# Experts in five teams of 128 token slots, with 4 KB and 8 KB weight runs

## The reference

```python
logits = xf @ router_w + router_b            # 256 tokens, 8 experts
top_logit, top_e = lax.top_k(logits, 2)
top_w = softmax(top_logit)
def expert_block(args):                      # D 1024, D_FF_EXPERT 3584
    tok_b, e = args
    xb = xf[tok_b]
    return (silu(xb @ wg[e]) * (xb @ wu[e])) @ wd[e]
out = zeros((T, D)).at[row_tok].add(y * row_w[:, None])
```

## Time and profile before

| | us |
|---|---|
| median of 3 runs (lowest, highest) | 1687.45 (1686.11, 1691.96) |
| the profiled execution, its own time | 1692.91 |
| its span, first to last instruction | 1691.1 |
| expert part: first weight load issued | 722.2 |
| first expert product | 732.7 |
| last down product's records end | 1676.0 |
| last addition into x ends | 1684.8 |

### The profile page before, as it was taken

How to read it: one execution, slowest core, us unless ns; L and a number is a source line. 1 busy time by engine, 2 the same in 40 slices (tenths; PEclk the granted TensorE clock), 3 DMA queues, 4 the chain that set the end, 5 groups by cost and what they waited for, 6 DMA issues and landing times.

```text
span 1691.1 us, 16145 instructions
## 1 busy us (share of the span) xinstructions
PE 1611.1 (95%) x6482; PEld 868.2 (51%) x6482; DVE 480.8 (28%) x953; ACT 199.0 (12%) x439; POOL 0.9 (0%) x7
## 2 busy tenths in 40 slices
PE   3999989999989999789999999999999999999997
PEld 2566755555546667554454444454444444444443
DVE  6577733434343644330110011100111000111002
ACT  1123230000011233200010000000000000000000
POOL 0000000000000000000000000000000000000000
PEclk9999899999999999789999999999999999999999
DMA  9935625888762100099999998999999989999993
GB/s 347 327 109 199 236 87 174 277 294 290 286 233 96 58 1 1 1 345 395 392 368 391 392 392 332 387 341 389 388 359 370 386 337 389 392 359 361 392 392 125
DMA packets 222010, 481.53 MB, mean 285 GB/s; under 512 B 15816, under 2 KB 33608, under 8 KB 221936
## 3 DMA queue, kind: packets, MB, share of 16 engines
q1 hardware_dynamic: 220488, 478.64, 76.8%
q10 hardware_dynamic: 1448, 1.84, 0.5%
HBM read 479.41 MB, written 1.06 MB: 284 GB/s over the span
## 4 chain that ended last, share of the span: by engine, by line
PE 91%; DMA 3%; DVE 2%; SPq 2%; ACT 1%; issue 1%; DVEq 0%; ACTq 0%
PE bank L1209 31%; PE bank L1238 16%; PE bank L1204 11%; PE bank L971 7%; PE bank L1230 6%; PE bank L962 4%; PE bank L1178 3%; PE bank L1216 2%; DMA ring<-in_ada_w 1%; DMA ring<-in_moe_wg 1%; PE bank L1284 1%; PE bank L1300 1%; PE bank L1098 1%; DVE ada_acc L1412 1%; PE bank L952 1%; SPq L607 1%
## 5 line engine op out<-in xcount | busy, mean ns | idle before, releaser
L1209 PE MATMUL bank<-ring,h_T 128*128 128x512 f32 (+1 forms) x896 | 355.3, 550 | 3.8 <-ACT h_T L727 1.3
L1238 PE MATMUL bank<-ring,m_qk_T 128*128 128x512 f32 x624 | 277.7, 597 | 0.7 <-ACT m_qk_T L843 0.7
L1209 PEld LDWEIGHTS bank<-ring,h_T 128*128 128x128 f32 x896 | 167.8, 191 | 165.2 <-issue 114.7
L1209 PE MATMUL bank<-ring,cmp_region 128*128 128x512 f32 x448 | 197.1, 593 | 0.0
L1238 PEld LDWEIGHTS bank<-ring,m_qk_T 128*128 128x128 f32 x624 | 116.2, 190 | 144.8 <-issue 140.9
L1763 DVE SCALAR_TENSOR_TENSOR m_s_region<-s_v,bank 128x512 f32<-128x512 f32 (+1 forms) x70 | 39.1, 558 | 489.8 <-ACT s_v L836 353.2
L836 ACT ACTIVATE s_v<-bank 128x512 f32<-128x512 f32 (+1 forms) x70 | 34.5, 493 | 997.5 <-PE bank L1209 654.1
L1209 PEld LDWEIGHTS bank<-ring,cmp_region 128*128 128x128 f32 x448 | 83.7, 190 | 99.6 <-issue 99.6
L1767 DVE SCALAR_TENSOR_TENSOR m_s_region<-m_s_region,bank 128x512 f32<-128x512 f32 (+1 forms) x70 | 39.1, 558 | 317.6 <-PE bank L1209 224.3
L971 PE MATMUL bank<-ring,h_T 128*128 128x512 f32 (+1 forms) x320 | 117.6, 517 | 0.0
L1204 PE MATMUL bank<-ring,h_T 128*64 128x256 f32 x896 | 102.4, 381 | 1.0 <-DVE m_s_region L1767 1.0
(11 more groups left out here) (314 smaller groups left out, 1022.0 us busy)
## 6 DMA issues: line engine op xcount, KB each, us to landing
ring<-in_moe_wg SPq DMA_DIRECT2D x56, 2048.0 KB, 9.7
ring<-in_moe_wu SPq DMA_DIRECT2D x56, 2048.0 KB, 15.5
ring<-in_moe_wd SPq DMA_DIRECT2D x56, 2048.0 KB, 19.1
ring<-in_ada_w SPq DMA_DIRECT2D x28, 1024.0 KB, 8.9
ring<-in_ada_w SPq DMA_DIRECT2D x10, 2048.0 KB, 14.4
ring<-in_w_in SPq DMA_DIRECT2D x10, 2048.0 KB, 12.1
ring<-in_ffn_wg SPq DMA_DIRECT2D x6, 1536.0 KB, 10.4
ring<-in_ffn_wu SPq DMA_DIRECT2D x6, 1536.0 KB, 9.4
```

What stands on the lines that cost most here:

```text
L1209: last = mm(ps[4 + part][:, 0:w], xT[st.into][:, k, 128 * st.tile:128 * st.tile + 128], view_at(slot, w)[:, k, :], start=k == 0, stop=k == ...
L1238: last = mm(ps[st.y + half][:, :], hbT[:, j % 2, 128 * q:128 * q + 128], down_at(st.slots[2], st.w)[:, q, 512 * half:512 * half + 512], st ...
```

## The change

1. Experts go in five **teams** that fill 128 slots: one expert (128), two (96 + 32), one (128), two (96 + 32), two (64 + 64), by rank of count (0), (2, 7), (1), (3, 6), (4, 5). Instead of two steps a unit, PE computes one team at a time; each product of a k-step is issued once for each lane of array columns: one lane of 128, or lanes of at most 64 (0 to 64, 64 to 96, 96 to 128 in the 96 + 32 teams; 0 to 64, 64 to 128 in the last).
2. Work goes in **stages** of two units (the last of one). Gate and up loads take 512 rows by 1024 columns (4 KB runs), down loads two neighbouring rows per partition (8 KB runs); the hidden columns are transposed with a stride of 2 to match. The number and size of loads stay: 168 of 2 MB.
3. The scatter weights tokens in the picks themselves (`onehot_weighted`), one bank at a time, four products a team; the gather is 128 columns wide; releases move into the products and the ACT and DVE steps; the pair loop on SP is unrolled. `OVER` is 4; slot ranks and capacities are set by POOL.
4. The first four modulation chunks are summed half on DVE (four slices), half on PE (four products of 512 columns against `cond` spread over 128 columns), with one product that adds DVE's half; DVE takes the diagonal of the result.

```diff
-OVER = 3
+OVER = 4
+TEAMS = (((0, 0, 128),), ((1, 0, 96), (2, 96, 128)), ((3, 0, 128),), ((4, 0, 96), (5, 96, 128)), ((6, 0, 64), (7, 64, 128)))
+SLOT_RANK, SLOT_CAP = (0, 2, 7, 1, 3, 6, 4, 5), (128, 96, 32, 128, 96, 32, 64, 64)
+SPANS = ((0, 2), (1024, 2), (2048, 2), (3072, 1))
...
+        self.lanes = [(m, a, min(a + (128 if c1 - c0 == 128 else 64), c1)) for m, (_, c0, c1) in enumerate(TEAMS[team])
+                      for a in range(c0, c1, 128 if c1 - c0 == 128 else 64)]
...
+    for j in range(len(STAGES) + 1):
+        if j < len(STAGES):
+            for part in range(2):
+                for piece in range(STAGES[j].units):
+                    add(STAGES[j], part, piece)
+        if j:
+            for unit in range(STAGES[j - 1].units):
+                add(STAGES[j - 1], 2, unit)
...
+            for n, (st, part, piece, m) in enumerate(MOE_LOADS):
+                e, slot = expert_id(st.team, m), n % RING
...
+                sp.wait_ge(ring_free[slot], FREED[slot] + n // RING)
+                if part == 2:
+                    f0 = st.f0 + 512 * piece
+                    sp.dma_start(ring[:, slot, :].rearrange("p (g n) -> p g n", g=2),
+                                 w[f0:f0 + 512, :].rearrange("(g p f) n -> p g (f n)", p=128, f=2)).then_inc(ring_full[slot], 16)
+                elif st.units == 2:
+                    sp.dma_start(wide_at(slot), w[512 * piece:512 * piece + 512, st.f0:st.f0 + 1024].rearrange("(k p) n -> p k n", p=128)).then_inc(ring_full[slot], 16)
...
+            for e in range(N_EXP):
+                do(nc.gpsimd.memset(slot_rank[:, e:e + 1], float(SLOT_RANK[e])))
+                do(nc.gpsimd.memset(slot_cap[:, e:e + 1], float(SLOT_CAP[e])))
...
+            def ada_half_product(c):
...
+                w = slot_view(i, 512)
+                for k in range(KC // 2, KC):
+                    mm(b[:, :], cond[:, k:k + 1].to_broadcast([128, 128]), w[:, k, :], start=k == KC // 2, stop=False)
...
+            def moe_up(j, part, between=None):
...
+                for piece in range(2):
+                    if piece < st.units:
+                        moe_loaded(pe, st, part, piece)
+                    for unit in range(st.units):
+                        b = ps[((4, 2), (5, 3))[part][unit]]
+                        for k in range(4 * piece, 4 * piece + 4):
+                            for n, (m, c0, c1) in enumerate(st.lanes):
...
+                                last = mm(b[c0:c1, :], xT[st.team % 2][:, k, c0:c1], w, start=k == 0, stop=k == KC - 1)
...
+            def moe_down(j):
...
+                    for half in range(2):
+                        for q in range(4):
+                            for n, (m, c0, c1) in enumerate(st.lanes):
+                                slot = moe_slot(st, 2, unit, m)
+                                last = mm(ps[half][c0:c1, :], hbT[:, unit, 128 * q + c0:128 * q + c1],
+                                          down_at(slot, 512)[:, q, 512 * half:512 * half + 512],
+                                          start=st.begin and unit == 0 and q == 0, stop=end and q == 3)
...
+            for j in range(len(STAGES) + 1):
...
+                if j < len(STAGES):
+                    moe_up(j, 0, between)
+                    moe_up(j, 1)
+                    beside(j, 2)
+                else:
+                    moe_turn(j - 1, 0)
+                if j:
+                    moe_down(j - 1)
...
+            def ada_half_sum(c):
...
+                do(TS(a, w[:, 0, :], cond[:, 0:1], None, ALU.mult))
+                for k in range(1, KC // 2):
+                    do(STT(a, w[:, k, :], cond[:, k:k + 1], a, ALU.mult, ALU.add), acc_ready if k == KC // 2 - 1 else None)
...
+                    do(TTop(diagonal, b[:, :].rearrange("p (q n) -> p q n", q=4), eye, ALU.mult), mod_evac)
+                    do(V.tensor_reduce(modc[:, 4 * c:4 * c + 4], diagonal, AX.X, ALU.add))
+                    do(TTop(modc[:, 4 * c:4 * c + 4], modc[:, 4 * c:4 * c + 4], prm(l, "ada_b")[:, 4 * c:4 * c + 4], ALU.add))
```

More of the change, by code:

```diff
@@ L270, with __init__ @@
 class Step:
-    def __init__(self, w, tile, y, loads, rounds, first, last, begin, end, half=False, into=0):
+    def __init__(self, w, tile, y, loads, rounds, first, last, begin, end):
         self.w, self.tile, self.y, self.loads, self.rounds = w, tile, y, loads, rounds
         self.first, self.last, self.begin, self.end = first, last, begin, end
-        self.half, self.ew, self.into = half, w // 2 if half else w, into
         self.slots = [n % (PRE if rounds is None else RING) for n in loads]
@@ L570, in down_at, with wide_at, moe_loaded, moe_slot @@
             return ring[:, slot, 0:(w // 128) * D].rearrange("p (f n) -> p f n", n=D)
+        def wide_at(slot):
+            return ring[:, slot, :].rearrange("p (k n) -> p k n", k=KC // 2)
+        def moe_loaded(eng, st, part, piece):
+            for m in st.members:
+                n = st.load[part, piece, m]
+                eng.wait_ge(ring_full[n % RING], 16 * (FILLED[n % RING] + n // RING + 1))
+        def moe_slot(st, part, piece, m):
+            return st.load[part, piece, m] % RING
+        def down_done(eng, st, unit):
+            n = st.load[2, unit, st.members[-1]]
+            eng.wait_ge(ring_free[n % RING], FREED[n % RING] + n // RING + 1)
         def step_loaded(eng, st, part):
@@ new lines, in moe_scatter @@
+            def moe_scatter(team, n, bank=7, added=True):
+                half, tt = divmod(n, 2)
+                pe.wait_ge(moe["y_1" if half else "y_0"], team + 1)
+                if n == 0:
+                    pe.wait_ge(moe["turn_evac"], team + 1)
+                if added and n:
+                    pe.wait_ge(moe["added"], 4 * team + n)
+                mm(ps[bank][:, :], pickT[team % 2][:, tt, :], ysb[:, 512 * half:512 * half + 512],
+                   start=True, stop=True).then_inc(moe["scattered"], 1)
@@ new lines, in _, with between @@
+            for j in range(len(STAGES) + 1):
+                def between(piece):
+                    if j and piece < STAGES[j - 1].units:
+                        moe_turn(j - 1, piece)
+                    beside(j, piece)
+                if j < len(STAGES):
+                    moe_up(j, 0, between)
+                    moe_up(j, 1)
+                    beside(j, 2)
+                else:
+                    moe_turn(j - 1, 0)
+                if j:
+                    moe_down(j - 1)
+                if j < len(STAGES):
+                    beside(j, 3)
@@ L1777, in picks_turned, with onehot @@
-            def picks_turned(f, n, count, do):
+                    doe(TS(pick[0][:, tt, :], cst("iota"), over_rank[:, tt, bass.ds(e, 1)], None, ALU.is_equal), over["onehot"] if tt else None)
+            def onehot(team):
+                for tt in range(TT):
+                    for at, c0, c1 in TEAMS[team]:
+                        do(TS(pick[0][:, tt, c0:c1], cst("iota")[:, 0:c1 - c0], rank[:, tt, at:at + 1], None, ALU.is_equal),
+                           moe["onehot"] if team == 0 and tt and c1 == 128 else None)
@@ L1808, in add_residual, with add_over @@
+            def add_over(half, column, count):
+                dve.wait_ge(over["scattered"], count)
+                for tt in range(TT):
+                    xs = x[:, tt, 512 * half:512 * half + 512]
+                    doe(STT(xs, ps[(2, 7)[tt]][:, :], wts[:, tt, bass.ds(column, 1)], xs, ALU.mult, ALU.add), over["added"] if tt else None)
             def add_residual(tt, half, y):
```

438 lines of the change are left out of this document (251 added, 187 removed).

## The result

The changed kernel takes 1934.45 us (median of four runs, 1933.85 to 1937.88) where the kernel before takes 1689.7 beside it. The ratio is 1.145, with a 95% interval of 1.142 to 1.149: slower by 245 us. The profiled execution took 1937.88 us for a span of 1935.9.

What follows compares the result with a forecast made beforehand. PE was taken as the bound, transfers a few per cent behind. PE's teams run to 1714, 37 loads to 1904, then the end: span 1921, time 1917 us, slower by 14%; own range 1885 to 1960, stated range 1630 to 1955.

Steps and rivals of the forecast that it cites:

- The mixed k-step: Teams 1 and 3: the 64-column tile and the two 32s stream one after the other, 1.98 us a k-step.
- the first rival: Everything overlaps: the 64-column tile runs beside the 32s, loads bind shared teams; 1637 us, faster by 3%; chance 0.28.
- The teams' starts: Expert part: team 0 ends at 884, team 1 at 1230, team 2 at 1385; team 4 begins at 1714.
- with seven loads resident of the 44 that are left: Team 4, from 1714: transfers bind for the other 37 loads at 5.14 us, 190 us, to 1904.
- The last products: Last down products after the final load: 6.9 us.
- the rest of the end: After the last products: multiply, two scatters and an addition 3.3 us, then 6.3 to the end.
- The longer runs: Expert loads: 4 KB gate and up runs, 8 KB down runs; 864 us in all, 29 less, mean 5.14 a load.
- The first modulation: First modulation, sums half on PE: ready at 39.5 to 43.8 against 42.0; taken as 0, range -2.5 to +2 us.
- Two at a time: Rival, shared teams: only two of three tiles stream together, 1.29 us a k-step; 1688 us, no change; chance 0.08.
- overflow pass: Rival, experts: if the seventh expert's count ran over its slots, one expert more, some 150 us; chance 0.02 with similar mishaps.
- Its sum for team 0: First single team: PE's products 147 us plus gather, 151 us in all, ending at 884.

Runs made afterwards that it cites:

- the sorted kernel: The changed kernel with all products of the 64-column tile first within a load, then those of the 32s; 1872.31 us in one run.
- lanes32: The changed kernel with the 96 rows cut into three 32-column tiles, so shared teams have four tiles of 32; 1658.82 us, ratio to the kernel before 0.981; 1652.87 run again.
- singles first: lanes32 with the teams in the order single, single, shared, shared, shared; 1674.19 us.
- the last experiment: lanes32 with a shared team first and the first seven expert loads issued, experts named as constants, before the router's order is known; 1637.60 us, ratio to the kernel before 0.968.

## Why the prediction was right, and where it was off

The direction, the mechanism and the size hold: 1917 forecast, 1934.45 measured, inside the forecast's own range of 1885 to 1960. The stated range, 1630 to 1955, reaches down to a kernel that is faster by 3%, so that the time lies inside it says little; the teams' starts below say more.

**The mixed k-step.** 1.98 was taken, 1.985 is measured. It was put together from the mLSTM head, where the mix is in array rows, and from the products that follow transposes. That those rows carry over to a mix in columns was the guess of the forecast, and the first rival stood on the other side of it. The trace of the changed kernel decides it, and the sorted kernel shows both of its terms apart: a change costs 0.13 in the mean, 0.15 into the 64 and 0.12 into the 32s, as was taken, and the sizes stream one after the other even where hardly any change is left. The Trainium skill ("TensorEngine Tiling (Array Packing)", key properties) has tiles operate independently and also has a change of tiling mode drain the engine; these runs bear out both, the first for tiles of one size (four of 32 in 0.88 us) and the second for tiles of two sizes, though their columns are apart.

**The teams' starts.** The prediction's own ends, less the last down products (16.5 or 7), put the starts of teams 1 to 4 at 877, 1214, 1378 and 1714; the chain has 875.5, 1212.8, 1376.9 and 1714.1. The first product came at 730.0, not 732.7, which is within the 8 us that two executions of lanes32 differ by ahead of the experts; and team 0 took 1.4 us more than counted.

**The stretch that was mis-sized is the last team's**, 12 of the 15 us that the span is off. The step was "with seven loads resident of the 44 that are left": 37 x 5.14 = 190, to 1904. The last load landed at 1916.3. The window from the team's start to that moment:

```profile
1714.10:1916.30 202.20, 173.82 (x728) 59.06 (x728) 13.79 (x20) 8.96 (x15) 0.00 (x0) 0.96 1.01 405
```

405 GB/s over 202.2 us are 39 loads of 2.10 MB and not 37, at 5.18 us each. So five of the 44 had landed, not seven, which is 10 of the 12 us; the other 2 are the slower first 6 us. After these the rate was as counted (408 GB/s from 1720 to 1916.3, 5.14 us a load). The queue of the changed kernel around 1714:

```profile
1665.35 33.42 SPq L733 DMA_DIRECT2D ring<-in_moe_wg  x4
1698.88 22.63 SPq L733 DMA_DIRECT2D ring<-in_moe_wu  x4
1721.69 7.69 SPq L730 DMA_DIRECT2D ring<-in_moe_wd  x2
```

and the windows of its transfers:

```profile
1708.00:1714.00 6.00, 6.00 (x20) 1.00 (x18) 0.00 (x0) 0.00 (x0) 0.00 (x0) 1.00 0.40 158
1714.00:1720.00 6.00, 6.00 (x30) 2.07 (x30) 0.00 (x0) 0.00 (x0) 0.00 (x0) 1.00 0.79 285
```

The last loads for the new team go out as slots come free, up to 1721, and just before the switch the queue moves 158 GB/s. A slot that is being read is not a slot that holds the next load: of the seven, five are ahead here. Counted in the same way, lanes32 has six ahead when team 1 and team 3 start, each after a single team, and two when team 2 starts, after a shared one: a ring that the loads bind is not quite empty either. The orders say the same from another side. lanes32 against singles first is one refill of the ring, 958.4 less 934.7 to 937.7, so 21 to 24 us, 4.0 to 4.6 loads, and from two ahead to six are four. The expectation had seven (36 us) as one bound and five (26) as the other, and even five was a little high.

**The last products** took 8.73 us where 6.9 was taken, and the rest of the end 10.7 where 9.6 was. For the first, the windows of the end show the granted clock (here after the last load has landed):

```profile
1916.50:1925.00 8.50, 8.50 (x32) 2.74 (x32) 0.69 (x1) 0.00 (x0) 0.00 (x0) 0.81 0.01 2
```

PE had been waiting, and its last stage runs partly at the lower of its two levels, 1.2 GHz. The 6.9 came from a stretch in which it never waited. In lanes32 the same stage took 10.02 at 0.70.

**The longer runs** were priced at 0.31 us a load and 29 us in all, and the price is confirmed for the two mixtures that were run (411 against 393 GB/s, 5.10 against 5.34 us a load). The forecast's sum only used it in the last team; the 29 us could never show in a kernel whose PE binds from 730 to 1714. In lanes32 they are worth 19.5 by the medians, 24 to 27 by the table. The Trainium skill's figure of about 358 GB/s for the HBM side ("DMA: Bandwidth & Descriptors", on where 436 GB/s comes from) is passed by every one of these windows.

**The first modulation** was taken at 0 with bounds of -2.5 and 2; the scale is computed at 40.66 where it was 42.03 in the kernel before, 1.4 us earlier, with its weights landing half a microsecond later. That lies within the 39.5 to 43.8 that were named. First the kernel before, then the changed one:

```profile
42.03 0.17 DVE L1432 SCALAR_TENSOR_TENSOR mod_scale<-mod_cols,par 128x8 f32<-128x8 f32 x1
```

```profile
40.66 0.17 DVE L1603 SCALAR_TENSOR_TENSOR mod_scale<-mod_cols,par 128x8 f32<-128x8 f32 x1
```

**The rivals.** That all overlaps is refuted by the 0.99 us between the tiles' starts, but its arithmetic can be tested on lanes32, where the tiles do overlap: it said 1637 and lanes32 takes 1652.9 to 1658.8. Its team ends of 876, 1066 and 1218 came out as 876.8, 1069.5 and 1224.7, and the last load at 1635.7 instead of 1624. Here the ring is not what was off. The last 411 us of loads:

```profile
1224.70:1635.70 411.00, 344.55 (x2111) 122.20 (x2110) 31.91 (x53) 19.16 (x33) 0.00 (x0) 0.93 1.01 404
```

These are 79 loads, as the rival had counted (37 and 42), but at 5.20 us each, not 5.14, which is 5 of the 12 us; team 1 lost 3 more by a like rate, and team 2 took 155 us where 152 was counted. Two at a time is refuted twice: the mixed k-step is 1.985, not 1.29, and four lanes of 32, which would take 1.72 by that rule, take 0.88. The trace shows no work between the last team and the end, so no overflow pass ran.

What the prediction did not see, and what cost it nothing here, is that the ring is nearly empty when the experts start (one load had landed by 730.0). Its sum for team 0 is PE's alone, and a single team forgives it.

## What to carry to other kernels

Let all products that are to share the array have tiles of one size, even if that means more of them: three tiles of 32 beside a fourth cost 0.88 us a k-step, one of 64 beside two of 32 cost 1.99. Count what a ring has ahead as its slots less those being read (five or six of seven here), and its refill from what a load-bound stretch leaves in it (two), so four loads; and look for the moment when its first load can be named at all: where the address depends on a result, the ring starts nearly empty, and the team or layer that needs few bytes for its products belongs there. The version that beats both kernels is the change with that one edit on tile sizes, 1652.9 to 1658.8 us, 2% below the kernel before; putting a shared team first has the same time, and what is left beyond it is the start of the loads, the 17 us of the last experiment, which would need a first expert that is known without the router.

## What was not expected of the hardware

Tiles of two sizes never stream beside each other, even with their columns apart: in every change of size in the shared teams the new record waits for the old one's end and 0.09 to 0.10 us more, 0.12 or 0.15 us with what follows, near the 0.15 and 0.19 of the earlier trace rows where the columns are shared. The granted clock falls around some of the waits in lanes32's shared teams: the same 64 records take 7.07 us without a wait and 8.67, at a granted clock of 0.81, after one of 2.42 us, though there are also 7.07 after a wait of 3.15. So a PE that waits for loads may also pay for the products after it. As I read it, that costs no time as long as the loads bind, and 1.8 to 3.1 us in the last stage of all, where they no longer do. And one kernel's own executions differ by up to 11 us. Between the two profiled ones 8 of these lie ahead of the experts, where a stretch of the first layer that the change doesn't touch had a granted clock of 0.91 in one and 0.98 in the other. That is more than the modulation, the 8 KB runs or the narrow tiles in the last team could have shown in the medians.
